# Forgetting attention: transposes three steps behind the scores, a third probability buffer, and the causal mask added by VectorE

## The reference, cut to what matters

```python
def forgetting_attention(q, k, v, f_logit):           # 8 heads x 64, S = 512, Q_BLOCK = 128
    F = cumsum(log_sigmoid(f_logit), axis=1)
    def block(args):                                   # 128 queries against all keys
        s = einsum('bhqd,bshd->bhqs', q_blk * Dh ** -0.5, k)
        s = s + F_blk[..., None] - F[:, :, None, :]
        s = where(pos_blk[:, None] >= k_pos[None, :], s, -inf)
        return einsum('bhqs,bshd->bqhd', softmax(s), v)
# beside it, fed by the same projection: q, k, v of a gated delta rule
qkv = causal_conv_silu(concatenate([gq, gk, gv]), gdn_conv_w)     # 12 tiles of 128 x 512
```

## Time and profile before

| | us |
|---|---|
| median of 3 runs | 1825.12 |
| the profiled execution | 1823.65 |
| its span | 1821.9 |
| TensorE busy (share of the span) | 1785.5 (98%) |
| VectorE busy | 1173.7 (64%) |
| ScalarE busy | 741.4 (41%) |
| GpSimd busy | 1309.0 (72%) |

### The profile page before, as it was taken

The page is one execution under the profiler, slowest core; times in us unless marked ns, Lnnn a source line. Parts: engine busy times, 40 slices in busy tenths (PEclk is TensorE's granted clock), DMA queues, the critical chain, the costliest instruction groups (busy, mean ns, idle before and its releaser), DMA issues.

```text
span 1821.9 us, 28331 instructions
## 1 busy us (share of the span) xinstructions
PE 1785.5 (98%) x10180; PEld 1520.4 (83%) x10180; DVE 1173.7 (64%) x1775; ACT 741.4 (41%) x1386; POOL 1309.0 (72%) x1188
## 2 busy tenths in 40 slices
PE   9999999999999999999999999999999999999998
PEld 7788888878878799998888866798876778999886
DVE  7977664249974798877017776574454189888731
ACT  5521111137762466652014267553413256565001
POOL 8976666767777798877667865453772688888775
PEclk9999999999999999999999999999999999999999
DMA  7022223232123323234223311101321222323421
GB/s 280 1 102 83 92 92 139 92 128 89 72 74 111 139 94 117 94 118 181 95 93 105 105 58 48 69 26 47 116 98 42 93 109 80 113 102 108 168 99 69
DMA packets 26014, 179.36 MB, mean 98 GB/s; under 512 B 2864, under 2 KB 2992, under 8 KB 6960
## 3 DMA queue, kind: packets, MB, share of 16 engines
q1 hardware_dynamic: 24176, 168.31, 25.9%
q10 hardware_dynamic: 1728, 9.58, 1.4%
HBM read 171.58 MB, written 6.29 MB: 98 GB/s over the span
## 4 chain that ended last, share of the span: by engine, by line
PE 82%; DVE 8%; ACT 4%; issue 3%; POOL 3%; DMA 1%; ACTq 0%; DVEq 0%; POOLq 0%
PE bank L484 12%; PE bank L485 12%; PE bank L486 12%; PE bank L1432 6%; PE bank L1434 6%; PE bank L1433 6%; PE bank L1902 2%; PE bank L1903 2%; PE bank L1904 2%; PE bank L522 1%; PE bank L524 1%; PE bank L523 1%; POOL weights_lo L762 1%; DVE x_mixed_lo L1608 1%; PE bank L3178 1%
## 5 line engine op out<-in xcount | busy, mean ns | idle before, releaser
L376 POOL TENSOR_TENSOR weights_lo<-raw_weights,weights_hi 128x512 fp32r<-128x512 f32 (+4 forms) x400 | 541.9, 1355 | 39.9 <-ACT weights_hi L395 7.4
L374 POOL TENSOR_SCALAR weights_hi<-raw_weights 128x512 fp32r<-128x512 f32 (+4 forms) x376 | 259.7, 691 | 317.8 <-PE bank L486 170.4
L484 PE MATMUL bank<-x_hi,weights_hi 128*128 128x512 f32 x688 | 271.5, 395 | 0.2
L486 PE MATMUL bank<-x_lo,weights_hi 128*128 128x512 f32 x688 | 267.9, 389 | 0.0
L485 PE MATMUL bank<-x_hi,weights_lo 128*128 128x512 f32 x688 | 267.8, 389 | 0.0
L484 PEld LDWEIGHTS bank<-x_hi,weights_hi 128*128 128x128 f32 x688 | 129.2, 188 | 28.1 <-POOL weights_lo L376 0.8
L485 PEld LDWEIGHTS bank<-x_hi,weights_lo 128*128 128x128 f32 x688 | 129.2, 188 | 26.9 <-issue 1.0
L486 PEld LDWEIGHTS bank<-x_lo,weights_hi 128*128 128x128 f32 x688 | 129.1, 188 | 27.0
L1434 PE MATMUL bank<-x_lo,weights_hi 128*128 128x256 f32 x432 | 122.4, 283 | 0.0
L1474 POOL TENSOR_TENSOR weights_lo<-temps,weights_hi 128x512 fp32r<-128x512 f32 x72 | 107.6, 1513 | 4.7 <-ACT weights_hi L1511 4.7
L1474 POOL TENSOR_TENSOR weights_lo<-raw_weights,weights_hi 128x512 fp32r<-128x512 f32 x72 | 97.7, 1360 | 13.1 <-ACT weights_hi L1511 12.9
(11 more groups left out here) (588 smaller groups left out, 5179.0 us busy)
## 6 DMA issues: line engine op xcount, KB each, us to landing
raw_weights<-in_ffn_seven SPq DMA_DIRECT2D x36, 1024.0 KB, 4.7
raw_weights<-in_a_ug SPq DMA_DIRECT2D x16, 1024.0 KB, 4.8
raw_weights<-in_b_in SPq DMA_DIRECT2D x12, 1024.0 KB, 4.8
raw_weights<-in_ffn_down SPq DMA_DIRECT2D x12, 1024.0 KB, 4.7
raw_weights<-in_ffn_down SPq DMA_DIRECT2D x7, 1408.0 KB, 5.9
raw_weights<-in_a_out SPq DMA_DIRECT2D x8, 1024.0 KB, 4.8
raw_weights<-in_ffn_up SPq DMA_DIRECT2D x8, 1024.0 KB, 4.7
raw_weights<-in_b_out SPq DMA_DIRECT2D x8, 768.0 KB, 4.2
```

The lines of the kernel that those rows point to most:

```text
L374: nc.gpsimd.tensor_scalar(hi, raw, 1.0, 0.0, ALU.mult, ALU.add).then_inc(S("units_hi"), 1)
L376: nc.gpsimd.tensor_tensor(lo, raw, hi.bitcast(F32), ALU.subtract).then_inc(units_ready, 1)
L484: nc.tensor.matmul(ps, wh, xh[:, k, :], start=k == 0, stop=False)
L486: last = nc.tensor.matmul(ps, wh, xl[:, k, :], start=False, stop=k == last_k)
```

## The change

- The bf16 mask matmul and its two operands (`IDENT_B`, `CAUSAL_B`, and the two ScalarE copies that make them) are gone. VectorE adds the fp32 mask `CM` to the last 128 columns of the score bank, in place, and then waits for that addition before it takes the maximum.
- Transposes of step j are issued in step j + 3 (`BEHIND = 3`). The last ones are placed by `turned_at`: 29 and 30 in step 32, 31 in step 33. ScalarE copies them one step after that. The two transpose banks stay two.
- `FP` has three buffers. The exponential of i waits for the transposes of i - 3 where it waited for those of i - 2. To make room, `F_SPLIT` and `F_Q` change places, and the first buffer lies over `F_SPLIT`.
- ScalarE's `act_query_again` moves from qt = 2 to qt = 0, right behind the first half of the key.

```diff
@@ operands and buffers
-        F_SPLIT = place("fox_f_split", ZAT, [SEQ], F32R)
-        F_Q = place("fox_f_queries", ZAT + 2, [SEQ], F32R)
+        F_SPLIT = place("fox_f_split", ZAT + 2, [SEQ], F32R)
+        F_Q = place("fox_f_queries", ZAT, [SEQ], F32R)
-        IDENT_B = place("ident_b", ZAT + 28, [P], BF16)
-        CAUSAL_B = place("causal_b", ZAT + 28.25, [P], BF16)
-        FP = place("fox_p", ZAT + 4, [2, SEQ])
+        FP = place("fox_p", ZAT + 2, [3, SEQ])
@@ act_mix_in
-            nc.scalar.activation(IDENT_B[:, :], IDENT[:, :], ACT.Copy).then_inc(S("mask_b"), 1)
-            act.wait_ge(*due("causal", 2))
-            nc.scalar.activation(CAUSAL_B[:, :], CM, ACT.Copy).then_inc(S("mask_b"), 1)
@@ new
+        BEHIND = 3
+        def turned_at(i):
+            if i < STEPS:
+                return [i - BEHIND] if i >= BEHIND else []
+            return [[STEPS - 3, STEPS - 2], [STEPS - 1], []][i - STEPS]
@@ pe_fox
-            pe.wait_ge(*due("mask_b", 2))
-                    nc.tensor.matmul(ps[:, n - P:n], IDENT_B[:, :], CAUSAL_B[:, :], start=False, stop=False)
-                j = i - 2
-                if 0 <= j < STEPS:
+                for j in turned_at(i):
-                        last = nc.tensor.transpose(PS[2 + j % 2][...], FP[:, j % 2, ...], IDENT[:, :])
+                        last = nc.tensor.transpose(PS[2 + j % 2][...], FP[:, j % 3, ...], IDENT[:, :])
@@ dve_fox
+            dve.wait_ge(*due("causal", 2))
+                    own_block = score_bank(i)[:, n - P:n]
                     dve.wait_ge(*due("fx_s", i + 1))
+                    nc.vector.tensor_tensor(own_block, own_block, CM, ALU.add).then_inc(S("fx_masked"), 1)
+                    dve.wait_ge(*due("fx_masked", i + 1))
@@ act_fox
-                j = i - 3
-                if 0 <= j < STEPS:
+                for j in turned_at(i - 1) if i else []:
-                    if i >= 2:
-                        act.wait_ge(*due("fx_t", i - 1))
+                    if i >= 3:
+                        act.wait_ge(*due("fx_t", i - 2))
-                elif qt == 2 and 1 <= h and h + 1 < FOXH:
-                    act_query_again(act, h + 1)
+                    if qt == 0:
+                        act_query_again(act, h + 1)
```

More of the change, by code:

```diff
@@ L166 @@
     *(_members(kind, ("fx", FOXH * TOK), ("ma", MH * TOK)) for kind in ("s", "nm", "e", "p", "t", "pt")),
-    [("b_xc_lo", KB), ("row_sel", 4), ("f_rows", 1), ("gb_split", 4), ("go_with_q", TOK), ("column_half", 1)], [("b_xc_hi", KB), ("row_ones", 2), ("mask_b", 2), ("f_placed", 4)],
+    [("b_xc_lo", KB), ("row_sel", 4), ("f_rows", 1), ("gb_split", 4), ("go_with_q", TOK), ("column_half", 1)], [("b_xc_hi", KB), ("row_ones", 2), ("f_placed", 4), ("fx_masked", FOXH * TOK)],
     [("beta_tanh", 1), ("a_exp", 1), ("rows_exp", 1)],
@@ L2574, in pe_fox @@
                     for kt in range(j % TOK + 1):
-                        last = nc.tensor.transpose(PS[2 + j % 2][:, kt * P:(kt + 1) * P], FP[:, j % 2, kt * P:(kt + 1) * P], IDENT[:, :])
+                        last = nc.tensor.transpose(PS[2 + j % 2][:, kt * P:(kt + 1) * P], FP[:, j % 3, kt * P:(kt + 1) * P], IDENT[:, :])
                     last.then_inc(S("fx_t"), 1)
@@ L2680, in act_fox @@
                     act.wait_ge(*due("fx_r", i))
-                    nc.scalar.activation(FP[:, (i - 1) % 2, 0:n], FP[:, (i - 1) % 2, 0:n], ACT.Copy, scale=SUMC[:, i - 1:i]).then_inc(S("fx_p"), 1)
+                    nc.scalar.activation(FP[:, (i - 1) % 3, 0:n], FP[:, (i - 1) % 3, 0:n], ACT.Copy, scale=SUMC[:, i - 1:i]).then_inc(S("fx_p"), 1)
                 if i < STEPS:
@@ L2684, in act_fox @@
                     act.wait_ge(*due("fx_nm", i + 1))
-                    if i >= 2:
-                        act.wait_ge(*due("fx_t", i - 1))
-                    nc.scalar.activation(FP[:, i % 2, 0:n], score_bank(i)[:, 0:n], ACT.Exp, bias=MXC[:, i:i + 1], accum_out=SUMC[:, i:i + 1]).then_inc(S("fx_e"), 1)
+                    if i >= 3:
+                        act.wait_ge(*due("fx_t", i - 2))
+                    nc.scalar.activation(FP[:, i % 3, 0:n], score_bank(i)[:, 0:n], ACT.Exp, bias=MXC[:, i:i + 1], accum_out=SUMC[:, i:i + 1]).then_inc(S("fx_e"), 1)
                 started, ended = tile_at(i, 0), tile_at(i, 2)
```

## The result

| | before | after |
|---|---|---|
| median, us (22 runs each) | 1824.61 (1823.31 to 1826.04) | 1828.22 (1825.71 to 1831.17) |
| span of the profiled execution | 1821.9 | 1825.9 |
| start of step 0 / of step 31 in the span | 1042.32 / 1152.92 | 1042.33 / 1157.26 |

The change makes the kernel slower: ratio 1.0018, 95% interval [1.0012, 1.0024], 3.6 us. I forecast 1.0 us faster, and the time lies 0.2 us above my range. Step 0 starts at the same moment in both, step 31 4.3 us later, so the loss is made inside the 32 steps.

A forecast was written before the change was run, and what follows sets the result against it. The prediction took the ScalarE and VectorE loop to bound steps 8 to 31. Start -0.4 and three rounds -0.6 made -1.0 us (4.6 of gains against 3.6 of masks): forecast 1824.1 us, range 1819.0 to 1828.0.

The forecast's parts named there:

- The loop of ScalarE and VectorE sets the pace: Steps 8 to 31: the two engines work in turns, and this loop, not TensorE's work, sets the pace.
- the transposes' gain is small because of the two banks: Transposing a step later still waits for a bank's copy; with the queries' copy gone, release comes 0.98 us earlier a round.
- The mask matmul costs 0.13 of a pair: TensorE's score pair: dropping the bf16 mask matmul saves 0.13 us, 3.4 us of TensorE work over the 32 steps.
- A mask costs 0.33: VectorE, ahead of the maximum: 0.30 us for the addition plus 0.03 before the maximum starts, bounds 0.20 and 0.46.
- The queries' copy moves off the path: ScalarE's second copy of the queries, in the loop at step 18, takes 0.65 us there and costs nothing in step 16.
- Sum for a round: Steps 12 to 20: release -0.98, smaller copies -0.33, score pair -0.13, three masks +0.99, giving -0.45 us, taken as -0.2.
- my sign 5: Expected sign in the trace: from the exponential of step 12 to that of step 20 about 28.8 us, against 29.04.
- The start: Steps 0 to 7: earlier release, score pairs and smaller copies outweigh the masks of steps 3 to 5, -0.4 us.
- my last sentence: Closing caveat: the forecast would be wrong also if the mask slows under GpSimd's traffic; no size given.
- Rival C: VectorE becomes the bound from the 14th mask on the path: slower, 1828.3 us (17 masks) or 1831.1 (all 32); chance 0.12.
- my 11: Masks counted on the path out of 32, at 0.33 us each: 3.6 us, at most 17 places and 5.6 us.
- The four gaps: TensorE's lost time: 1.7 us a round, three times (the first 2.5), plus 1.75 in step 7, given as 7.8 us.

The follow-up runs named there:

- behind_three: The kernel before with only the transposes three steps behind and three probability buffers: 1824.18 us, ratio 0.9998.
- after_spaced: The changed kernel with one added wait: GpSimd splits tile t's first weight unit only after VectorE's taps of tile t - 3: 1820.70 us, ratio 0.9979.
- mask_on_vector: The kernel before with the mask added by VectorE and nothing else changed: 1830.52 us, ratio 1.0034.
- tensor_spaced: The changed kernel with the mask back as TensorE's matmul and an added wait that keeps GpSimd's split off the taps: 1819.43 us, ratio 0.9966.
- queries_spaced: The kernel before with the queries' copy moved and an added wait that keeps GpSimd's split off the taps: 1819.38 us, ratio 0.9973.
- after_light: The changed kernel with GpSimd's split of the delta rule's projection weights cut to 8 columns a unit: 1818.74 us, ratio 0.9969.

## Why the prediction was wrong, point by point

- **The loop of ScalarE and VectorE sets the pace, and the transposes' gain is small because of the two banks.** Right as far as the runs go: the wait names the copy, and behind_three shows a gain of 0.2 us where a full release was in sight. Even my 0.98 a round was too much for it alone. That a third bank would free it wasn't tried.
- **The mask matmul costs 0.13 of a pair.** Right. In step 15 the pair takes 0.46 after (1094.48 to 1094.94), 0.59 before. Up to step 6 the changed kernel is 0.98 us ahead.
- **A mask costs 0.33, from the lines of the earlier trace rows.** Right: 0.293, and the maximum starts 0.03 to 0.04 after its end, as my rows had it. What the semaphore alone costs between the two isn't shown, as no run has this pair without it.
- **The queries' copy moves off the path.** Right, and undersized (3.8 us for 1 to 1.5).
- **"Sum for a round": this is the step that failed.** It took every other duration in the loop as fixed, VectorE's taps too, and so put what GpSimd's split does to them at nothing. From the exponential of step 12 to that of step 20 it is 30.47 us after (my sign 5 said 28.8) and 29.04 before; with GpSimd's split cut short it is 27.57 and 28.13. So the schedule alone is 0.56 us shorter (I had 0.2), and the split costs 2.9 us a round in the changed kernel, the slow clock behind it included, and 0.9 in the kernel before. That turns the round into 1.4 longer; the next one is 1.5 longer. The start failed in the same way: I had it 0.4 us shorter, but step 8 begins 0.2 later than before and step 12 1.3 later (1083.23 and 1081.90); with the split cut short in both, step 12 begins 0.6 earlier, counted from step 0. I had the taps' row in the same table from which I took the maximum, with a mean of 0.86 against 0.75 for the same operation undisturbed, and didn't ask why; my last sentence thought of GpSimd only for the mask, which it doesn't slow.
- **Rival C** had the sign and the engine, at a chance of 0.12, but another mechanism: it counted masks on the path. The worth of all masks with the split off the taps is that of eight, fewer than my 11 and far from the 14 from which it was to decide. By my sign (a round longer than 29.1) it was C.
- **The long wait's second price** was in none of my cases: the slow clock, by the estimate above some 1.2 of the 4.3 us lost by step 31.
- **Slips in the working, none of them decisive.** The four gaps add up to 7.65 us, not 7.8. The total counts the start (steps 0 to 7) and three rounds, though the first round overlaps the start, and it holds 12 masks where I had counted 11. And the range ends at 1828.0 as "C's lower case", which the prediction itself puts at 1828.3.

The Trainium skill has the rule that I should have weighed. "Perfetto Trace Analysis", section "Optimizing Scalar/DVE Operations", says that GpSimd and VectorE share an SBUF read port. The traces agree with it: taps, gates and rests, with two SBUF operands, go from 0.69 to 0.75 up to 1.8; the read of a tile and the mask, with one, stay at 0.69 and 0.29 in all kernels. The queries' rest took 1.01 beside the split in before and 0.69 beside it in after_spaced, and that fits one shared reader too, since it began second in the one and first in the other. The port itself no run looks at.

## What to carry to other kernels

Moving one engine's work by a microsecond moves it against the others' too; before costing a change at fixed durations, look for groups whose mean lies above the least of the same form, find what runs beside them, and ask whether it will still be there. An added wait can be a gain: an engine with slack can be held back until the one in the loop has passed. And look for the buffer that is waited for last, here the transposes' bank, before enlarging another; that a third bank would pay is my guess, no run has it.

## What the runs showed of the hardware

- A tap (128x512 fp32, both tensors in the SBUF) takes 0.74 to 0.75 us alone and up to 1.8 when it begins while GpSimd's split runs (two operations of 128x512, 0.62 and 1.3 to 1.6 us in before and after). A 128x512 read from a bank with one SBUF operand takes 0.69 in both cases.
- TensorE's granted clock stood at 0.50 for some 3.4 us from within or soon behind idle gaps of 2.7 to 3.0 us (steps 19 and 27 here, 7, 19 and 27 in mask_on_vector), and matmuls of 512 columns stood 0.43 us apart there. But the gap of 3.03 us in step 11 of the changed kernel left it at 1.00, as did gaps of up to 1.95 us in behind_three: the length of the gap alone doesn't tell.
- It also stood at half outside the attention, in other places from one execution to the next: 0.52 and 0.50 in before from 1452 to 1460 us, which the page's digits of 9 (90% or more) don't show, and 0.60 in tensor_spaced from 1220 to 1224 us where queries_spaced has 1.00.
- The added masks took 0.292 to 0.294 us on the mean in after, after_light, mask_on_vector and after_spaced, whatever ran beside them.
